# First modulation by pairs of k-tiles, with the products of three chunks of w_in begun on each pair

## What is computed

```python
mod = silu(c) @ w_ada + b_ada                     # c: 1 x 2048, w_ada: 2048 x 12288
shift1, scale1, gate1, shift2, scale2, gate2 = split(mod, 6)
h = rms_norm(x, norm1_w) * (1 + scale1) + shift1
proj = h @ w_in                                   # 2048 x 8192: pool, q, k, v, g_a, g_b
```

## Time and profile before

| | |
|---|---|
| median of 3 runs | 2414.98 us |
| the profiled execution | 2406.36 us, span 2405.1 us |
| TensorE busy | 2253.9 us (94%) |
| VectorE busy | 1528.9 us (64%) |
| ScalarE busy | 1084.0 us (45%) |
| GpSimd busy | 297.4 us (12%) |
| moved by DMA | 468.52 MB, mean 195 GB/s |
| mean granted TensorE clock | 0.969 of full |

### The profile page before, as it was taken

The page is one execution under the profiler, slowest core; times in us unless marked ns, Lnnn a source line. Parts: engine busy times, 40 slices in busy tenths (PEclk is TensorE's granted clock), DMA queues, the critical chain, the costliest instruction groups (busy, mean ns, idle before and its releaser), DMA issues.

```text
span 2405.1 us, 27296 instructions
## 1 busy us (share of the span) xinstructions
PE 2253.9 (94%) x10579; PEld 1803.2 (75%) x10579; DVE 1528.9 (64%) x2050; ACT 1084.0 (45%) x1566; POOL 297.4 (12%) x374
## 2 busy tenths in 40 slices
PE   5789999999898999999999998999998879999998
PEld 1267878877687888888888886788887767877776
DVE  6878778878877645645655655565654435676664
ACT  1054445643346543543543545555545413555543
POOL 6633221123322100100100000000000000000000
PEclk9899999999999999999999999999999989999999
DMA  9887856678877756756756654444446433333333
GB/s 333 291 282 267 279 182 220 214 226 276 265 251 244 231 192 211 237 192 208 236 187 215 222 175 158 158 141 149 149 145 205 136 110 123 123 99 112 106 123 123
DMA packets 225268, 468.52 MB, mean 195 GB/s; under 512 B 13850, under 2 KB 19188, under 8 KB 224500
## 3 DMA queue, kind: packets, MB, share of 16 engines
q1 hardware_dynamic: 196944, 388.78, 48.6%
q0 software_dynamic: 20480, 67.13, 8.6%
q10 hardware_dynamic: 7716, 10.88, 1.3%
HBM read 464.65 MB, written 2.10 MB: 194 GB/s over the span
## 4 chain that ended last, share of the span: by engine, by line
PE 86%; DVE 7%; DMA 2%; ACT 2%; issue 2%; POOL 0%; ACTq 0%; DVEq 0%
PE banks L571 25%; PE banks L573 24%; PE banks L572 24%; PE banks L582 2%; DVE ada_acc_vec L1514 2%; PE banks L832 2%; PE banks L844 1%; DMA ada_w<-in_w_ada 1%; DVE ada_acc L1467 1%; PE banks L858 1%; PE banks L859 1%; PE banks L857 1%; PE banks L922 1%; DMA raw<-in_w_ada 1%; DMA x<-in_x 0%
## 5 line engine op out<-in xcount | busy, mean ns | idle before, releaser
L1446 DVE TENSOR_TENSOR w_low<-raw,w_high 128x1024 fp32r<-128x1024 f32 x674 | 821.6, 1224 | 597.4 <-ACT w_high L1013 596.3
L1013 ACT CAST w_high<-raw 128x1024 fp32r<-128x1024 f32 x674 | 701.2, 1047 | 798.5 <-PE banks L573 797.7
L571 PE MATMUL banks<-w_high,act_a_high 128*128 128x512 f32 (+1 forms) x1696 | 686.5, 405 | 14.3 <-DVE w_low L1446 8.4
L573 PE MATMUL banks<-w_high,act_a_low 128*128 128x512 f32 (+1 forms) x1696 | 665.6, 392 | 0.0
L572 PE MATMUL banks<-w_low,act_a_high 128*128 128x512 f32 (+1 forms) x1696 | 664.6, 392 | 0.0
L571 PEld LDWEIGHTS banks<-w_high,act_a_high 128*128 128x128 f32 x1696 | 324.9, 192 | 92.4 <-issue 22.0
L573 PEld LDWEIGHTS banks<-w_high,act_a_low 128*128 128x128 f32 x1696 | 323.8, 191 | 69.2
L572 PEld LDWEIGHTS banks<-w_low,act_a_high 128*128 128x128 f32 x1696 | 325.0, 192 | 61.8
L438 POOL DMA_DIRECT2D ada_w<-in_w_ada x256 | 186.8, 730 | 953.4 <-DVE ada_acc L1467 947.2
L571 PE MATMUL banks<-w_high,act_b_high 128*128 128x512 f32 x640 | 250.6, 392 | 0.8 <-DVE act_b_low L1671 0.8
L573 PE MATMUL banks<-w_high,act_b_low 128*128 128x512 f32 x640 | 249.6, 390 | 0.0
(11 more groups left out here) (336 smaller groups left out, 2213.9 us busy)
## 6 DMA issues: line engine op xcount, KB each, us to landing
raw<-in_w_ff SPq DMA_DIRECT2D x128, 1024.0 KB, 5.2
raw<-in_w_in SPq DMA_DIRECT2D x64, 1024.0 KB, 6.6
ada_w<-in_w_ada POOLq DMA_DIRECT2D x256, 256.0 KB, 5.0
raw<-in_b_w_in SPq DMA_DIRECT2D x44, 1024.0 KB, 5.0
raw<-in_a_w_in SPq DMA_DIRECT2D x36, 1024.0 KB, 5.1
raw<-in_w_ada SPq DMA_DIRECT2D x32, 1024.0 KB, 7.2
raw<-in_w_o SPq DMA_DIRECT2D x16, 1024.0 KB, 7.3
raw<-in_a_w_out SPq DMA_DIRECT2D x16, 1024.0 KB, 5.2
```

What stands on the lines that cost most here:

```text
L571: T.matmul(out, xh, wh, start=(c.first and k == 0), stop=False)
L573: last = T.matmul(out, xl, wh, start=False, stop=(c.last and k == c.nk - 1))
L1013: A.copy(WH[:, h % SPL, :, :], split_ap(h)).then_inc(*done("high", h))
L1446: V.tensor_tensor(WL[:, h % SPL, :, :], split_ap(h), WH[:, h % SPL, :, :].bitcast(F32), ALU.subtract).then_inc(*done("low", h))
```

## The change

The first modulation is now made in 8 rounds, one for each pair of k-tiles of x. A round i loads the 256 columns of shift1 and of scale1 of that pair in four slots of 4 k-tiles (two DMAs of 512 KB a slot, rows of 1 KB) into buffers of their own, `ada_first0` to `ada_first3`, the last of which lies where `ada_w` is. VectorE does three of the four k-tiles (`first_vec`), TensorE the fourth with the weights as the stationary operand and one column moving (`first_pe`); GpSimd's part is gone, the row copies and turns too. `first_sum` adds over partitions into PSUM, and `first_mod` makes that pair's scale and shift. As soon as a pair is modulated the products of the chunks ("in", 0), ("in", 1) and ("in", 2) for these two k-tiles are begun, with three PSUM pairs, and the units and halves of these three chunks are taken in turn. The work of round i + 1 of the modulation is written between the products of round i. The bands and the first `ada_w` piece move to chunk 3. The pieces lie on in (5), ga and ua (8), gb and ub (8), wo (3) and f1 (8), and are summed in the next chunk at a given k-tile, always in bank 3.

```diff
+EARLY = 3
+FIRST_RING = 4
...
+PLACES = ([("in", n) for n in range(EARLY, 8)] + [(name, n) for n in range(4) for name in ("ga", "ua")]
+          + [(name, n) for n in range(4) for name in ("gb", "ub")] + [("wo", n) for n in range(3)])
+DUE_STEP = {"in": 4, "ga": 5, "ua": 6, "gb": 4, "ub": 4, "wo": 4, "f1": 4}
...
     def sync_program(S):
+        def first_load(i, u):
+            if i > 0:
+                S.wait_ge(*of("first_pe", (i - 1, u)))
+                S.wait_ge(*of("first_vec", (i - 1, u, 2)))
+            for m_ in range(2):
+                S.dma_start(first[u][:, :, m_, :], first_w[:, u * UK:(u + 1) * UK, m_, i * AC:(i + 1) * AC]).then_inc(*landed(f"first_landed{u}", i))
...
+        for i in range(KT // 2):
+            for u in range(FIRST_RING):
+                if i % 2 == 0 and u == (2 if i else FIRST_RING):
+                    for n in range(EARLY):
+                        unit_load(i // 2 * EARLY + n)
+                first_load(i, u)
...
     def tensor_program(T):
+        def first_pe(i, u):
+            T.wait_ge(*of(f"first_landed{u}", i))
...
+            for j in range(4):
+                mm = T.matmul(sum_cols(i)[:, j:j + 1], first[u][:, UK - 1, j // 2, j % 2 * P:(j % 2 + 1) * P],
+                              cT[:, (u + 1) * UK - 1:(u + 1) * UK], start=(u == 0 and j == 0), stop=False)
+            mm.then_inc(*done("first_pe", (i, u)))
+
+        def first_sum(i):
+            T.wait_ge(*of("first_vec", (i, FIRST_RING - 1, 2)))
+            for j in range(4):
+                mm = T.matmul(sum_cols(i)[:, j:j + 1], acc_v[:, i % 2, j * P:(j + 1) * P], ones[:, 0:1],
+                              start=False, stop=(j == 3))
+            mm.then_inc(*done("first_summed", i))
...
+        for i in range(KT // 2):
+            more = i + 1 < KT // 2
+            for n in range(EARLY):
+                if more:
+                    first_pe(i + 1, n)
+                if n == 0:
+                    T.wait_ge(*of("a_low", ("in", i)))
...
+                for k in (2 * i, 2 * i + 1):
+                    mm_tile(C["in", n], k, STAT["in"])
+            if more:
+                first_pe(i + 1, FIRST_RING - 1)
+                first_sum(i + 1)
...
     def vector_program(V):
+        def first_mod(i):
+            ks = slice(2 * i, 2 * i + 2)
+            V.wait_ge(*of("first_summed", i))
+            V.tensor_tensor(mod1[:, :, ks], sum_cols(i).rearrange("p (m k) -> p m k", m=2), bias1[:, :, ks],
+                            ALU.add).then_inc(*done("mod1_sum", i))
+            V.wait_ge(*of("mod1_sum", i))
+            V.tensor_tensor(mod1[:, 1, ks], mod1[:, 1, ks], norm1[:, ks], ALU.mult).then_inc(*done("mod1_made", i))
...
+        for i in range(KT // 2):
+            more = i + 1 < KT // 2
+            for n in range(EARLY):
+                if more:
+                    first_vec(i + 1, n)
+                if n == 0:
+                    modulate("in", 2 * i, tmp0)
...
+                rest(EARLY * i + n + AHEAD)
+            if more:
+                first_vec(i + 1, FIRST_RING - 1)
+                first_mod(i + 1)
...
             for k in range(8):
                 rests(C["ua", n], k)
+                ada_tiles(C["ua", n], k)
+                ada_keep(C["ua", n], k)
...
     def scalar_program(A):
+        for i in range(KT // 2):
+            for n in range(EARLY):
+                cast(EARLY * i + n + AHEAD)
+                if i == KT // 2 - 1 and n > 0:
+                    in_take(n - 1)
+            if i + 1 < KT // 2:
+                first_modulate(i + 1)
```

More of the change, by code:

```diff
@@ L123, in add @@
         every.append(c)
+        return c
+    def add(*args, **more):
+        c = define(*args, **more)
+        for i in range(c.nk // c.per // 2):
+            take_unit(c, i)
+            for sub in range(2):
+                take_half(c, c.units[i], sub)
     def add_outputs(name, w):
@@ L132, in weight_stream @@
     w_in = t["w_in"][0]
[L133 to L137, removed]
+    cols = [CH * i + part * POOL_W for i in range(2) for part in (0, 3, 1, 2)]
+    early = [define(("in", n), w_in, 0, cols[n], KT, n) for n in range(EARLY)]
+    for i in range(KT // UK):
+        for c in early:
+            take_unit(c, i)
+        for sub in range(2):
+            for c in early:
+                take_half(c, c.units[i], sub)
+    for n in range(EARLY, 8):
+        add(("in", n), w_in, 0, cols[n], KT, n % 2)
     for n in range(4):
@@ L406, in sync_program @@
[L406 to L421, removed]
+        first_w = t["w_ada"][0].rearrange("(k p) (m n) -> p k m n", p=P, n=D)
@@ L451, in pool_program @@
         power(NT, "x", 0)
[L452 to L465, removed]
-                G.wait_ge(*of("pro_pool_scaled", w))
-                G.wait_ge(*of("pro_pool", w - 1))
-                G.tensor_tensor(acc_g[:, n, :], acc_g[:, n, :], r[:, 3, :], ALU.add).then_inc(*done("pro_pool", w))
         def chunk_loads(name, bands=False):
@@ L512, in pool_program @@
             chunk_loads(("ub", n))
-        for n in range(4):
+        for n in range(3):
             chunk_loads(("wo", n))
@@ L1449, in rests @@
             if k % c.per == 0:
[L1450 removed]
+                rest(c.halves[k // c.per] + AHEAD)
         def ready(c):
[L1453 removed]
+            return of("used", c.halves[-1])
         def ada_tile(p, a):
@@ L1494, in vector_program, with first_vec @@
         V.tensor_scalar(cT[:, :], cT[:, :], 0.5, None, ALU.mult).then_inc(*done("cT_made"))
+        def first_vec(i, u):
+            acc_ = acc_v[:, i % 2, :]
+            V.wait_ge(*of(f"first_landed{u}", i))
+            for kk in range(UK - 1):
+                w, c_ = first[u][:, kk, :, :].rearrange("p m n -> p (m n)"), cT[:, u * UK + kk:u * UK + kk + 1]
+                if (u, kk) == (0, 0):
+                    if i == 0:
+                        V.wait_ge(*of("cT_made"))
+                    if i >= 2:
+                        V.wait_ge(*of("first_summed", i - 2))
+                    V.tensor_scalar(acc_, w, c_, None, ALU.mult).then_inc(*done("first_vec", (i, u, kk)))
+                else:
+                    V.wait_ge(*of("first_vec", (i, u, kk - 1) if kk else (i, u - 1, UK - 2)))
+                    V.scalar_tensor_tensor(out=acc_, in0=w, scalar=c_, in1=acc_, op0=ALU.mult,
+                                           op1=ALU.add).then_inc(*done("first_vec", (i, u, kk)))
@@ L1557, in vector_program, with heads_norm @@
         qn8 = qn[:, :, :].rearrange("p a (h d) -> p (a h) d", d=P)
-        for n in range(8):
+        def heads_norm(n):
             c = C["in", n]
-            if n == 1:
+            V.wait_ge(*of("heads_squared", n))
+            V.tensor_reduce(ss[:, 0:8], qn8, AX, ALU.add).then_inc(*done("heads_sums", n))
+            V.wait_ge(*of("heads_sums", n))
+            mean(8, P, 1e-6, "heads", n)
+            V.wait_ge(*of("rms_inverse", ("heads", n)))
+            V.tensor_tensor(qn8, pair[c.pair].rearrange("p a (h d) -> p a h d", d=P),
+                            rs[:, 0:8].unsqueeze(2).broadcast_to([P, 8, P]), ALU.mult).then_inc(*done("pair_free", c.name))
+        heads_norm(2)
+        for n in range(EARLY, 8):
+            c = C["in", n]
+            if n == EARLY:
                 V.wait_ge(*of("pool_fill", "count"))
```

377 lines of the change are left out of this document (167 added, 210 removed).

## The result

The changed kernel took 2420.3 us, the median of 14 runs (2413.4 to 2430.7), and the kernel before 2412.2 in the 14 runs beside them: a ratio of 1.0038, 95% interval 1.0022 to 1.0053. It is slower by 8 us by the medians and 9 by the ratio, where 7 us gained were forecast. The profiled executions are 2406.36 us before (span 2405.1) and 2413.42 after (span 2412.2), the shortest of its 14.

A forecast was written before the change was run, and what follows sets the result against it. Prologue bound by w_ada loads and VectorE, the rest by TensorE with VectorE close behind. 26.7 - 6.1 - 14.4 + 0.5 = 6.7 us gained: 2399.7 for the profiled execution, forecast 2408, range 2388 to 2425.

The forecast's parts named there:

- Part 1: Prologue: without GpSimd's share, VectorE's multiply-adds, 1343 ns on average before, come 0.82 us apart, 9.8 us a round.
- Part 2: Loop of one round: VectorE, TensorE and ScalarE wait in turn; 18.0 us with low clock at each start, 15.8 without.
- Part 3: A round's loads of w_ada and w_in: 16.7 us at 333 GB/s, hidden below 18.0; 19.1 at 280 GB/s as bound.
- Part 4: First round: first product at 41 us, end at 56.7; after six more rounds E = 178, 26.7 us gained.
- E: Time when chunk ("in", 2) ends on TensorE and ScalarE's first Square starts: 204.6 us before, 178 forecast.
- the ring: Order of waits among VectorE, TensorE and ScalarE setting a round's length: 18.0 us at low clock, 15.8 at high.
- rival 1: Early rounds: the clock stays high, the round is 15.8 us, E 163, the time 2393; chance 0.20.
- rival 3: Early rounds: loads of 1 KB rows at 280 GB/s bind, 19.1 us a round, E = 187, the time 2417; chance 0.13.
- rival 4: Early rounds: loads don't overlap, each pays its start alone, 32 us a round, E = 262, the time 2492; chance 0.03.
- Part 5: Bands moved from chunk 1 to chunk 3: TensorE stands some 9.2 us, net 6.1 us lost (bounds 3 and 10).
- Part 6: Pieces moved into ua: 7.4 us VectorE work each, period 39.4 to 43, four times, 14.4 us lost (bounds 10, 29).
- Rival 2: Ga and ua: VectorE sets the pace, none of its idle time is absorbed, 29.5 us lost, the time 2423; chance 0.17.

The follow-up runs named there:

- the filler: 10 added 512-column products a round into a PSUM bank nobody reads, against the changed kernel: rounds of 16.0 us, 2416.4 us.
- run 5: Changed kernel with VectorE's fourth slot of a round written ahead of its third subtraction: 17.2 us a round, 2422.5 us.
- run 4: Changed kernel with the filler: E = 163.3 us, the kernel 2416.4 us.
- Run 3: Changed kernel with the bands made in chunk 5 instead of chunk 3: chunks 3 to 7 in 117.0 us, the kernel 2414.2 us.
- run 9: Changed kernel without the four pieces in ua (loads, operations and sums left out): last Square to y_b_high 182.0 us, the kernel 2394.7 us.
- run 2: Changed kernel with VectorE's key copy moved ahead into ua and the value copy to ga's k-tile 7: last Square to y_b_high 197.0 us, kernel 2407.6.
- run 8: Changed kernel with the early key copy and the ga and ua piece operations spread over 24 k-tiles: last Square to y_b_high 198.0 us, kernel 2412.8.
- run 10: Four kernels: the changed one with key and value copies early on ScalarE, bands in chunk 5 and varying further edits: 2399.2, 2400.5, 2392.9 and 2392.8 us.

## Why the prediction was wrong

**Part 1 was right,** though its reading wasn't: seven operations in 6.57 us are 0.94 us each, not 0.82. The first of them, with GpSimd at work beside it, took 1.64 us, and the six behind it, without, 0.75 each and 0.82 apart. After the change they are 0.77 apart.

**Parts 2 to 4 were right in mechanism and too dear.** First product 39.2 (forecast 41), first round ended at 53.1 (56.7), rounds 17.0 (18.0), E 168.4 (178). The low clock at each round's start is there, and the filler shows that the high one gives 16.0 (15.8). The Trainium skill ("TensorE: Matmul & The Clock Gate", HAM oscillation) has a loop that waits for its next slice start each one at the low clock, and the trace agrees in that (granted clock 0.50 to 0.53 in the first 3.5 us of products of all seven rounds behind the first), but not in the cause that the page tells of: TensorE waited for no load there and ran one-column matmuls until 2.14 us before (2.95 in the last). What the ring missed is that TensorE's own row of 36 products and small matmuls is as long as VectorE's; run 5 shows it. Loads were hidden, and nearer to binding than 16.7 of 18.0 suggests: 5.76 MB at the 358 GB/s of run 4 are 16.1 us of 17.0. Rivals 1, 3 and 4 fell. The price that the Trainium skill ("DMA: Bandwidth & Descriptors", Anatomy of one DMA) gives in rival 4 is the page's for DMAs issued by GpSimd; these are SyncE's, and no run had them without overlap.

**Part 5 failed in two steps.** One is a slip in the sum: the 3.1 us that the bands cost in chunk 1 were already in the difference of E, so the loss to enter was 9.2 us, not 6.1. The other is the size: 13.0 us. TensorE, which before was busy for all of the 113.7 us, stood 3.6 us for the turn of chunk 3's heads, 3.1 us in two waits for `w_low` and 1.0 in two small ones, 7.7 in all, and came back at the low clock, to which the other 5.3 us go:

```profile
207.37 1.97 PE L606 MATMUL banks<-ident,qn 128*128 128x128 f32 x8 [3.64 <-DVE qn L1620]
```

```profile
168.40:295.10 126.70, 118.96 (x514) 96.96 (x513) 101.53 (x149) 50.25 (x52) 46.72 (x60) 0.96 0.78 255
195.00:215.00 20.00, 15.59 (x58) 12.30 (x57) 16.35 (x27) 6.47 (x7) 8.94 (x12) 0.80 0.58 195
209.33:213.00 3.67, 3.67 (x11) 2.79 (x10) 3.60 (x6) 0.69 (x1) 1.17 (x2) 0.50 0.88 268
```

The clock was charged in Part 2 and forgotten here. Run 3, which only moves the bands, gives 9.7 of the 13.0 us back.

**Part 6 was the step that decided.** "Period 43, 3.6 more, four times: 14.4", with 29 as the upper bound; the stage lost 30.8 us, 27.0 of them by the pieces, and these made the wait for `y_b_low` 5.5 us longer besides (run 9). "Late next is `pair_copied`" was written down and priced at nothing. It is a ring: a late VectorE stops TensorE, TensorE's scores come later and slower, and VectorE waits for what follows from them. So `z_log` did not go "partly", it grew from 1.9 to 3.6 us a period; this ring is 12.0 us of the loss (run 2). The rest is VectorE's time of 40.3 us with 3 to 4 us of waits that no order removed (runs 2, 8 and 10), and the 3.8 us that aren't the pieces'. `y_b_low` had no term in the sum.

Rival 2 said that VectorE sets the pace and that nothing of its idle time is absorbed. By its own mark, a loss of 27 us in the stage, it is what came in, with 29.5 for 30.8. But its waits were to stay as they were, and what happened is that one of them went to TensorE and came back larger. That its 2423 us lies so near the 2420.3 is partly luck: it shares a gain at E that is 9.5 us too small and bands that are 6.9 us too cheap, and these errors nearly cancel.

With the measured terms the sum is 36.2 - 13.0 - 30.8 + 1.3 - 0.8 = -7.1, where the forecast had +6.7: E was 9.5 us better, the bands 6.9 worse and the stage 16.4 worse.

**Open.** Shortening VectorE's work by 4 us a period when the ring was gone gave 2.5 us in the stage, and spreading the loads 4.4 more; each is near what two executions differ by, both together (6.9) are not. How much of the last 15 us belongs to VectorE's work and how much to the loads isn't settled finer than that. The gb and ub stage took some 5 us less in the profiled execution of the changed kernel than in most others (266 to 269 from `y_b_high` to `ff_tmp` in eleven of them); that fits its lying 7 us under the median. The traces show where: TensorE's four waits for `qT` there are 9.1 us in the changed kernel and 12 to 15 in those eleven. Why they were short isn't shown.

## What to carry to other kernels

When an engine that was 84% busy (33.1 of 39.4 us) gets the work that fills it, don't add the work to its period: list what stands behind it in its queue, who waits for that, and whether what this one makes comes back to the first engine. A ring is worth what comes back to the engine that sets the pace: without it VectorE waited 11.7 us less for `z_log` and the stage took 12.0 less, while the 17.9 us that TensorE no longer stood don't add to that. Work that another engine waits for belongs ahead of work that nobody waits for. An edit's credit and its charge must be read between the same two marks.

## What the runs showed of the hardware

- TensorE's clock fell although TensorE was busy with one-column matmuls up to 2.14 us before (the row at 107.16); with 10 products of 512 columns added in each round it stayed at full (1.00 in the round from 85.47). In one of the rounds it was low up to 141 us all the same (mean 0.81), with TensorE busy 18.25 of 18.25 us.
- A multiply-add on 8 columns costs 0.27 us where one on 256 costs 0.48, so cutting columns doesn't take away the operation.
- Loads with rows of 1 KB and 2 KB mixed ran at 357 to 359 GB/s with the DMA engines full, between the two bounds of Part 3.
